# New order of the first loads, K units in pairs with four homes, and an earlier choice of the second group's pages, in a hybrid decoder layer on one Trainium2 core

## What is computed

```python
rq, rk, rv, rg, mq, mk, mv = project(ys, norm1_g[layer], w_in[layer], pos_s)
ret_o, s_s = retention_chunked(rq, rk, rv, state_ret[layer].astype(jnp.float32), chunk_s)
...
k_past = ck[pages].reshape(past_len, MOBA_HEADS, MOBA_HD).astype(jnp.float32)
...
gate = jnp.einsum('qhd,hnd->qhn', qf, k_mean)
_, top_i = lax.top_k(gate, k_sel)  
...
s = jnp.einsum('qhd,qhjkd->qhjk', qf, kg) * scale
p = jax.nn.softmax(s.reshape(qb, h, -1), axis=-1).reshape(s.shape)
return jnp.einsum('qhjk,qhjkd->qhd', p, vg)
...
u = tok @ wgu + bgu
a = glu * jax.nn.sigmoid(SWIGLU_ALPHA * glu) * (lin + 1.0)
return acc + g[:, None] * (a @ wd + bd), None
```

## Time and profile before

| | us |
|---|---|
| median of 3 runs | 1238.06 |
| lowest and highest | 1237.89, 1240.36 |
| span of the profiled execution | 1237.4 |
| PE busy | 1197.3 (97%) |
| DVE busy | 382.1 (31%) |
| ACT busy | 239.5 (19%) |
| POOL busy | 68.3 (6%) |
| DMA, mean | 405 GB/s, 500.6 MB |

### The profile page before, as it was taken

One profiled execution on the slowest core, in us unless ns is written; L12 is line 12 of the kernel. 1 busy time (PEld: TensorE's weight loads), 2 busy tenths in 40 slices (PEclk: granted clock), 3 DMA queues, 4 the chain that ended last, 5 costly groups with the idle time before them and its releaser, 6 DMA issues.

```text
span 1237.4 us, 17275 instructions
## 1 busy us (share of the span) xinstructions
PE 1197.3 (97%) x7264; PEld 508.4 (41%) x7264; DVE 382.1 (31%) x555; ACT 239.5 (19%) x560; POOL 68.3 (6%) x70
## 2 busy tenths in 40 slices
PE   6999999999999999999999999999999999999997
PEld 3455544635443434344343434344343434343432
DVE  4999955434311111221111111122111111111122
ACT  4021144504111101121111101021111111110103
POOL 2222202230000000000000000000000000000000
PEclk9999999999999999999999999999999999999999
DMA  8999889999899999999999999999999999999995
GB/s 335 384 361 363 331 331 383 365 384 389 365 421 427 428 427 427 431 427 430 427 430 429 427 431 426 431 427 430 428 427 430 427 430 427 429 429 427 428 427 209
DMA packets 49978, 500.64 MB, mean 405 GB/s; under 512 B 5656, under 2 KB 6320, under 8 KB 19088
## 3 DMA queue, kind: packets, MB, share of 16 engines
q1 hardware_dynamic: 42416, 430.56, 83.2%
q0 software_dynamic: 7520, 69.47, 14.2%
HBM read 495.29 MB, written 4.72 MB: 404 GB/s over the span
## 4 chain that ended last, share of the span: by engine, by line
PE 66%; DMA 21%; DVE 7%; issue 4%; ACT 2%; SPq 0%; DVEq 0%; ACTq 0%
PE psum L1028 24%; DMA arena<-w_gate_up 18%; PE psum L1059 14%; DVE arena L1582 6%; PE psum L936 6%; DMA arena<-w_down 3%; PE psum L956 3%; PE psum L534 3%; PE psum L942 2%; PE psum L754 2%; PE psum L968 2%; PE psum L625 2%; PE psum L454 2%; PE psum L975 1%; PE psum L1095 1%
## 5 line engine op out<-in xcount | busy, mean ns | idle before, releaser
L1028 PE MATMUL psum<-arena 128*64 128x512 f32 x1920 | 421.7, 594 | 11.6 <-DMA arena<-w_gate_up 11.5
L1028 PEld LDWEIGHTS psum<-arena 128*64 128x64 f32 x1920 | 135.0, 137 | 294.6 <-issue 267.8
L1931 DVE TENSOR_SCALAR arena<-psum 128x512 f32<-128x512 f32 x32 | 22.2, 692 | 675.1 <-PE psum L1028 635.7
L1059 PE MATMUL psum<-arena 128*64 128x512 f32 x960 | 212.6, 595 | 0.0
L1185 ACT ACTIVATE arena<-psum 128x512 f32<-128x512 f32 (+3 forms) x190 | 96.2, 509 | 350.3 <-PE psum L1059 170.7
L1582 DVE STREAM_TRANSPOSE arena<-arena 128x2048 f32<-128x2048 f32 x32 | 121.2, 3940 | 2.0 <-PE psum L519 1.9
L1059 PEld LDWEIGHTS psum<-arena 128*64 128x64 f32 x960 | 66.2, 137 | 124.3 <-issue 122.5
L534 PE MATMUL psum<-arena 128*128 128x512 f32 x224 | 107.3, 616 | 0.4 <-ACT arena L1185 0.4
L1455 ACT ACTIVATE arena<-arena 128x512 f32<-128x512 f32 x30 | 18.9, 631 | 412.4 <-DVE arena L1931 412.4
L1185 ACT ACTIVATE arena<-psum,arena 128x128 f32<-128x128 f32 (+2 forms) x162 | 49.1, 401 | 173.6 <-PE psum L534 113.4
L936 PE MATMUL psum<-arena 128*128 128x128 f32 x512 | 76.9, 293 | 0.2 <-DVE arena L1843 0.2
(11 more groups left out here) (264 smaller groups left out, 712.1 us busy)
## 6 DMA issues: line engine op xcount, KB each, us to landing
arena<-w_gate_up SPq DMA_DIRECT2D x128, 2048.0 KB, 31.0
arena<-w_down SPq DMA_DIRECT2D x63, 2048.0 KB, 32.9
arena<-w_in SPq DMA_DIRECT2D x7, 2048.0 KB, 18.4
arena<-w_out SPq DMA_DIRECT2D x2, 2048.0 KB, 12.9
out<-arena POOLq DMA_DIRECT2D x1, 2048.0 KB, 19.8
arena<-w_down SPq DMA_DIRECT2D x2, 1024.0 KB, 38.8
out<-arena SPq DMA_DIRECT2D x3, 512.0 KB, 3.3
arena<-x_prompt SPq DMA_DIRECT2D x2, 512.0 KB, 5.4
```

Of the source, the lines that this page charges most:

```text
L1028: last = mm(psum[64 * g:64 * (g + 1), b, :], xt[:, 2 * kk + m, lhs], gate_slot[slot][:, m, c:c + 512], start=False, stop=kk == 3 and m == ...
L1059: last = mm(psum[64 * g:64 * (g + 1), 2, :], at_sb[:, m, SLOTS * q:SLOTS * (q + 1)], down_slot[slot][:, m, 512 * g:512 * (g + 1)], start=q ...
```

## The change

SP's order becomes: page table, first constants, sample rows, prompt tiles 0 and 1, block 0 in two halves, blocks 1 and 2, tables, block 3. The four gains go to ACT's queue, and ACT loads the square root table ahead. On DVE the row numbers of K come before the gains' copy, those of V and the first turned unit before the reciprocal of x's norm. POOL asks for K units 0 and 1 at once and for unit 2 when all of block 0 has landed. On PE most `stay_awake` calls go, and `prompt_part(0, 0)` stands before `sample_part(0)`, its first four matmuls on the first half of the block. Turned K gets two more homes (free columns at 12288 and 14336, where V set 2 lands later, which therefore waits for the last scored unit). The queries are spread by 16 copies of twice the size. K units stand in pairs at the places of `K_AT`, the last one in block 5, tile 0. On DVE `choose(1)` stands ahead of the prompt's normalising, and the rotation of k and `q_dec` behind it; on ACT `probabilities(1)` stands between the tiles of block 6, and the places of `evacuate_scores` follow the new places of the units.

```diff
-        kt_sb = at(DN, 2, 4 * 512)
+        KT_AT = (DN, DN + 2048, 12288, 14336)
...
-        UNITS_IN = (3, 3, 3, 3, 3, 4, 3, 3, 4, 3, 0, 0, 0, 0)
+        K_AT = {(0, 1): (5,), (1, 0): (2, 7), (1, 1): (5,), (2, 0): (1, 5), (2, 1): (2, 7), (3, 0): (1, 7),
+                (3, 1): (4,), (4, 0): (0, 6), (4, 1): (4,), (5, 0): (1, 6)}
...
             for tile in range(2):
-                stay_awake(5, 2)
                 pe.wait_ge(x_in[tile], 16)
...
-            stay_awake(5, 2)
             pe.wait_ge(x_scaled, 1)
             n_x = transposes(A, [x_sb[0:NS, 2, k * P:(k + 1) * P] for k in range(KC)], NS)
+            stay_awake(5, 2)
...
+                if tile == 0:
+                    pe.wait_ge(*((win_in[b % 3], 16 * (b // 3 + 1)) if b else (block0_half, 16)))
...
+                    if b == 0 and tile == 0 and k == 4:
+                        pe.wait_ge(win_in[0], 16)
...
-                    for u in range(first + units * k // KC, first + units * (k + 1) // KC):
-                        k_unit(u)
+                    if k in K_AT.get((b, tile), ()):
+                        k_unit(units_done[0])
+                        k_unit(units_done[0] + 1)
+                        units_done[0] += 2
...
+            prompt_part(0, 0)
             q_bank = A.bank()
-            stay_awake(5, 2)
             mark["q_sample"] = (a_full, sample_part(0), q_bank)
-            prompt_part(0, 0)
...
+            act.dma_start(gain_in[0:8, :], t["norm1_g"][0].rearrange("(k p) -> k p", p=P)).then_inc(gains_in, 16)
...
+            nc.scalar.activation(stat[:, 63:64], stat[:, 62:63], ACT.Sqrt)
...
-                    if u >= 2:
-                        dve.wait_ge(k_scored, u - 1)
...
+                    if u >= 4:
+                        dve.wait_ge(k_scored, u - 3)
...
+                if u == 2:
+                    pool.wait_ge(win_in[0], 16)
...
-                elif n > 2:
+                elif n == 2:
+                    pool.wait_ge(k_scored, K_UNITS)
+                else:
                     pool.wait_ge(v_used, n - 2)
...
+            sp.dma_start(win[:, 0, 0:4], first[:, 0:4]).then_inc(block0_half, 16)
+            sp.dma_start(win[:, 0, 4:8], first[:, 4:8]).then_inc(win_in[0], 16)
```

More of the change, by code:

```diff
@@ L239, in build_kernel, with kt_sb, qk_heads @@
         k_raw = at(KV, 4, 4 * 512)
+        def kt_sb(u):
+            return at(KT_AT[u % 4], 4 * 512)
+        def qk_heads(c):
+            both = at(Q + 2304 + 128 * c, 2, 512)[:, :, 0:160].rearrange("p g (u r) -> p g u r", u=2)
+            return both[:, :, :, 0:64].rearrange("p g u (w x) -> p g u w x", w=2)
         HT = cur; cur += 2304
@@ L437, in build_kernel @@
         V_SETS = PAGES
-        UNITS_IN = (3, 3, 3, 3, 3, 4, 3, 3, 4, 3, 0, 0, 0, 0)
-        assert sum(UNITS_IN) == K_UNITS
+        K_AT = {(0, 1): (5,), (1, 0): (2, 7), (1, 1): (5,), (2, 0): (1, 5), (2, 1): (2, 7), (3, 0): (1, 7),
+                (3, 1): (4,), (4, 0): (0, 6), (4, 1): (4,), (5, 0): (1, 6)}
+        assert 2 * sum(map(len, K_AT.values())) == K_UNITS
         @block.tensor
@@ L522, in k_unit @@
                 last.then_inc(k_scored, 1)
+            units_done = [0]
             def prompt_part(b, tile, amid=None):
[L526 to L529, removed]
+                if tile == 0:
+                    pe.wait_ge(*((win_in[b % 3], 16 * (b // 3 + 1)) if b else (block0_half, 16)))
                 w = win[:, b % 3]
@@ L1556, in evacuate_t @@
                                         psum[:, V.bank(), 0:4 * w].rearrange("p (c w) -> p c w", c=4)))
-            evacuate(gain, width=28)
+            dve.wait_ge(consts_in, 16)
             dve.wait_ge(pages_in, 16)
@@ L1565, in _ @@
             ins.then_inc(k_rows_ready, 1)
+            evacuate(gain, width=28)
             dve.wait_ge(x_rms, 1)
@@ L1570, in _, with k_transposes @@
             evacuate_scaled(h_t, P, 1, range(4, 8), gain)
+            link(v.tensor_tensor(v_pages, page_all.rearrange("p (n m) -> p n m", m=8),
+                                 const("page").unsqueeze(1).broadcast_to([P, 2 * SEQS, 8]), ALU.mult))
+            link(v.reduce_sum(v_first, v_pages, axis=AXX))
+            v.tensor_scalar(v_rows, v_first, const("lane")[:, 1:2], None, ALU.add).then_inc(v_rows_ready, 1)
+            def k_transposes(first, last):
+                for u in range(first, last):
+                    dve.wait_ge(k_in[u % 4], 16 * (u // 4 + 1))
+                    if u >= 4:
+                        dve.wait_ge(k_scored, u - 3)
+                    v.transpose(kt_sb(u).rearrange("p (e b r) -> p r e b", e=16, b=32),
+                                k_raw[:, u % 4, :]).then_inc(k_trans, 1)
+            k_transposes(0, 1)
             dve.wait_ge(x_rms, 2)
@@ L1574, in _ @@
             dve.wait_ge(zeroed, 2)
-            def k_transposes(first, last):
-                for u in range(first, last):
-                    dve.wait_ge(k_in[u % 4], 16 * (u // 4 + 1))
-                    if u >= 2:
-                        dve.wait_ge(k_scored, u - 1)
-                    v.transpose(kt_sb[:, u % 2, :].rearrange("p (e b r) -> p r e b", e=16, b=32),
-                                k_raw[:, u % 4, :]).then_inc(k_trans, 1)
-            k_transposes(0, 1)
+            k_transposes(1, 2)
             q_full, q_n, q_bank = mark["q_sample"]
@@ L1708, in _ @@
             v.tensor_scalar(pm[:, 16:32], pm[:, 0:16], -SCALE, None, ALU.mult).then_inc(p_bias, 1)
[L1709 to L1713 removed]
+            choose(1)
             dve.wait_ge(p_exp, 1)
```

55 lines of the change are left out of this document (22 added, 33 removed).

## The result

The change makes the kernel slower: 1252.61 us median of 4 runs (1250.85 to 1255.64), against 1238.53 (1237.89 to 1240.36) for the kernel before, measured beside it. The ratio is 1.0112, with a 95% interval of 1.01 to 1.0125, so 14 us lost where 15 were forecast as a gain. The profiled execution spans 1253.8 us (before: 1237.4).

The account below looks back on a forecast made before the run. The expert weight stream over DMA was taken as the bound, its uninterrupted start set by the front. Gains of 14.0 (parts 1 to 3) and 2.4, less 1.4, gave 15.0 us: 1238.06 to 1223 us, range 1216 to 1231.

Parts of the forecast that it names:

- a microsecond taken off the front comes off the total: Work before the expert stage: time saved there shortens the whole run equally, provided the front's own transfers still fit.
- still 56.0 and then 58.7 us apart: Expert stage: a sign that expert pairs keep their old spacing, first 56.0 us, later 58.7 us.
- gave it nothing on the path: Front on TensorE: removed matmuls only kept it busy, without path gain; lower clock could add up to 4 us.
- Part 1: First loads: K asked for earlier, so unit 2 is turned from 28.8 us instead of 33.4; gain 4.6 us.
- Part 2: Turns of K: four homes and pairs remove VectorE's 1.95 us wait on TensorE; gain 1.9 us.
- Part 3: TensorE behind the last K unit: 7.8 us of work already done, tie costs 0.3; running gain 14.0 us.
- Part 4: Second group's choice moved ahead: TensorE's 1.42 us wait for exponentials goes, clock adds 1; gain 2.4 us.
- the hiding argument: Within part 4: later rotations hide behind TensorE's other work, ScalarE's 3.9 us of exponentials between block 6's tiles.
- Part 5: Retention state comes late as its reader moves earlier and the next V set shares its flow; loss 1.4 us.
- a wait of more than 3 us before the state is read: Retention stage: a sign that would show the prediction wrong, TensorE waiting over 3 us for the state.
- The slower one: Rival: the change makes the kernel slower; chance 0.05, its size not in the text given.
- the four: Rivals: late start with starved w_in (0.22), better than the sum (0.17), no effect (0.05), slower (0.05).

Follow-up runs that it names:

- the healed one: The change plus 48 already met semaphore waits (24 counted instructions) at the start of TensorE's program: 1230.23 us, ratio 0.9941 to the kernel before.
- +40 and +128: The change with 128 or 304 met waits at TensorE's start, loop 40 or 128 instructions past the kernel before's place: 1238.41 and 1248.87 us.
- -12 and 0: The change with 24 or 48 met waits at TensorE's start, loop 12 instructions before or at the kernel before's place: 1232.36 and 1230.23 us.

## Why the prediction was wrong, point by point

**The expert stage.** The step that failed is "a microsecond taken off the front comes off the total", with its sign that the pairs would be "still 56.0 and then 58.7 us apart". It holds only while TensorE's loop costs what it did. The four returns cost 27.4 us of waits and some 3 us each (2.8 to 3.6) of low clock behind them, 40 us. Three pairs now take 177.6 to 179.0 us (474.0 to 653.0, 653.0 to 831.1, 831.1 to 1008.7), and three pairs at the DMA's pace 3 x 58.7 = 176.1: the bound of this stage went from the weights to TensorE. The waits for weights vanished (11.5 us in the list of before; with their low clock 2.7 us in each of the later pairs), and 24.1 us net were lost. The six matmuls were judged by what they do on TensorE ("gave it nothing on the path"), which the runs bear out in the kernel before (1.0002 with waits in their place), and not by the room they take in the program. The source had a function named `place_loop` in front of me. What it emits turned out to be nothing, but its name is the warning.

What the traces show of the fetching is this. The packets are of 16 KB (1.11 MB in 68), nine for each return in the changed kernel, and TensorE waits 1.8 to 2.4 us at the return and 4.2 to 5.0 us a matmul later. At the place of the kernel before, the loop runs from 520 to 1060 us, three returns, without one packet. Why a place 24 instructions earlier needs them no run shows, and neither do the runs show the length of the body from which I had estimated that only few places are bad.

**Part 1** was right within its bounds. K was asked for at 6.06 us (forecast 6.5), and unit 2, which waits for block 0, at 20.3 (block 0 forecast at 19.8). Unit 2 was turned from 30.12 and not 28.8, and what it waited for was the queries and not its own landing: the sample rows were done at 26.5 us and not 25.0, and the sixteen copies of q took 3.22 us and not 2.6. The gain is 3.3 us and not 4.6.

**Part 2** was right: no wait in the turns, 143.9 us for the last turn (142.2 forecast, the 1.3 above and 0.4 more).

**Part 3** gave 11.1 of 14.0 us at the second transposes:

```profile
144.37 2.29 PE L526 MATMUL psum<-arena 128*32 128x128 f32 x64
146.59 7.99 PE L543 MATMUL psum<-arena 128*128 128x512 f32 x18
154.51 1.95 PE L509 MATMUL psum<-arena 128*32 128x128 f32 x64
...
157.69 0.49 PE L464 MATMUL psum<-arena 128*128 128x128 f32 x2 [0.59 <-ACT arena L1195]
```

The term mis-sized is what stands behind the last turn: the pair was scored 2.7 us after the last turn (143.9 to 146.6), and I had charged 1.2 for a single unit. With the 1.7 us of part 2 that is the difference, within 0.3.

**Part 4** was wrong in sign, as it stands in the change. The wait for the exponentials did go, as forecast. But the old order had also held V set 11 back by 3 us, which kept it off the state's last packets. The step that failed is in the hiding argument: I named who covers the moved work, and did not follow which transfer TensorE's earlier arrival would start.

**Part 5** was mis-sized: 1.4 us, bounds 0 to 3; measured 6.0 us of wait in the change and 8.1 in the healed one. The sign that I had named, a wait of more than 3 us before the state is read, was there. I had named the two parties, the state and the next V set, and had treated their meeting as a loss of share. It is a matter of when the set starts: 29.2 us to landing with the set 13.0 us behind the state's issue, 20.4 and 20.2 with the set 14.5 and 21.0 us behind. Parts 1 to 3 alone, with loop and state in order, give 1.18% (the version with part 4 undone), 14.6 us; 14.0 had been forecast for them.

**The rivals.** The slower one, to which I had given 0.05, was a low clock on TensorE from the missing matmuls. It had the right edit and the wrong mechanism: stretch 30 to 40 us has a clock of 1.00 in the healed version without them and 0.78 before. In the kernel before it falls to 0.70 without them (with the waits in their place), and the time stays the same. None of the four said where the time went, and 0.05 for slower was too little for a change that shortens the program ahead of a long loop.

## What to carry to other kernels

Look at the instruction queue's row before and after any edit ahead of a long hardware loop, even one that only deletes work: packets in the middle of the loop where another version has none (here 27 against none from 520 to 1060 us) came with eight waits of 27.4 us in all, and 24 instructions of met waits ahead of the loop took 1252.6 us to 1230.2. Check that filler leaves an instruction, by the instruction count of the profile. When an engine is made earlier, list the transfers that its earlier arrival starts, and ask which transfer still under way they will overtake; the best start of V set 11 was neither the earliest (210.23 us) nor one behind the state's landing (217.87), but 215.48.

## What the runs showed of the hardware

- With the loop's body unchanged, a return costs 7 us of waits and some 3 us of low clock at one place of the body (24 instructions before the old one), 1.9 to 2.4 us of waits at two others (+40 and +128), and at two more (-12 and 0) nothing is fetched and nothing lost. Some 16 of the 40 us that the four returns cost fell on time in which TensorE had waited for weights before; 24 showed. What decides between 7 and 2.4 us of waits is open, and so are what makes a place good or bad and the length of the body.
- 48, 128 and 304 met waits at the start of the program raised the count of instructions by 24, 64 and 152. They held TensorE for 4.9 us (64 instructions) and 14.3 us (152), 77 to 94 ns per instruction.
- A strided load (the state; 397 packets for 0.81 MB, so 2 KB each, beside V packets of 16 KB) moved mostly when GpSimd's queue was nearly empty: 0.17 MB in 3 us beside it (201 to 204 us, 83 of its packets and 72 of the other queue's), 0.81 MB in 3 us without (210 to 213 us). A set issued 13.0 instead of 14.5 us behind it moves its end by up to 9 us, and splitting the load over two queues leaves that end where it was (28.3 us).
- Not settled: whether the state's last packets wait in one engine or in all. No view of the trace tells the engines apart.
